# Queries and keys of the latent attention made in token rows and turned on TensorE, with the key products between the two halves of the value products

## What is computed

```python
def mla_shared_kv(h, w_kv_a, kv_a_norm, w_kv_b, k_nope_norm, k_rope_norm, cos, sin):
    ckv = h @ w_kv_a
    c_kv = rms_norm(ckv[..., :256], kv_a_norm)
    k_rope = apply_rope(rms_norm(ckv[..., 256:], k_rope_norm), cos, sin)
    kv = (c_kv @ w_kv_b).reshape(bsz, seq, 16, 64 + 64)
    k_nope, v = rms_norm(kv[..., :64], k_nope_norm), kv[..., 64:]
    k = concatenate([k_nope, broadcast_to(k_rope, (bsz, seq, 16, 32))], -1)
...
def mla_queries(h, w_q_a, q_a_norm, w_q_b, q_nope_norm, q_rope_norm, cos, sin):
    c_q = rms_norm(h @ w_q_a, q_a_norm)
    q = (c_q @ w_q_b).reshape(bsz, seq, 16, 64 + 32)
    q = concatenate([rms_norm(q[..., :64], q_nope_norm),
                     apply_rope(rms_norm(q[..., 64:], q_rope_norm), cos, sin)], -1)
...
s = q_block @ k.T / sqrt(96);  p = softmax(causal(s));  o = p @ v
```

## Time and profile before

| | us |
|---|---|
| median of three runs | 1800.92 (1800.91 to 1801.32) |
| the profiled execution's own time | 1800.97 |
| its span, first to last instruction | 1799.2 |
| first query product of the attention stage starts | 599.46 |
| first transpose of probabilities of head 0 | 629.96 |
| last score block (head 15) starts its causal term | 767.22 |

### The profile page before, as it was taken

The page is one execution under the profiler, slowest core; times in us unless marked ns, Lnnn a source line. Parts: engine busy times, 40 slices in busy tenths (PEclk is TensorE's granted clock), DMA queues, the critical chain, the costliest instruction groups (busy, mean ns, idle before and its releaser), DMA issues.

```text
span 1799.2 us, 27385 instructions
## 1 busy us (share of the span) xinstructions
PE 1755.8 (98%) x10262; PEld 1417.5 (79%) x10262; DVE 1234.6 (69%) x1863; ACT 931.8 (52%) x1668; POOL 488.0 (27%) x383
## 2 busy tenths in 40 slices
PE   9999999999999999999999999999999999999997
PEld 6778799999887656678999988778666777866675
DVE  8964488887446677758888835465676576567657
ACT  6634466654224677646566522232567633366763
POOL 0870267674000000006776600122000213200010
PEclk9999999999999999999999999999999999999999
DMA  6322322323333111122323233333111133312111
GB/s 217 91 90 82 94 95 95 118 95 118 95 97 95 40 32 29 59 82 72 117 95 118 93 117 89 96 96 97 59 59 48 48 93 100 101 47 59 49 60 56
DMA packets 58799, 152.64 MB, mean 85 GB/s; under 512 B 17024, under 2 KB 22048, under 8 KB 58672
## 3 DMA queue, kind: packets, MB, share of 16 engines
q1 hardware_dynamic: 55120, 148.24, 26.5%
q0 software_dynamic: 3552, 2.70, 0.6%
HBM read 143.76 MB, written 4.19 MB: 82 GB/s over the span
## 4 chain that ended last, share of the span: by engine, by line
PE 84%; DVE 6%; ACT 4%; POOL 3%; issue 2%; DMA 0%; SPq 0%; ACTq 0%; DVEq 0%; POOLq 0%
PE bank L2420 11%; PE bank L2421 11%; PE bank L2422 11%; PE bank L2633 8%; PE bank L2635 7%; PE bank L2634 7%; PE bank L2989 3%; PE bank L2991 3%; PE bank L2990 3%; PE bank L2942 2%; PE bank L2971 2%; PE bank L2972 2%; PE bank L2973 2%; PE bank L2713 1%; DVE wl L1532 1%
## 5 line engine op out<-in xcount | busy, mean ns | idle before, releaser
L1532 DVE TENSOR_TENSOR wl<-raw,wh 128x1024 fp32r<-128x1024 f32 (+3 forms) x199 | 234.1, 1176 | 271.3 <-ACT wh L831 266.9
L831 ACT ACTIVATE wh<-raw 128x1024 fp32r<-128x1024 f32 (+3 forms) x199 | 193.0, 970 | 354.1 <-PE bank L2422 287.6
L2420 PE MATMUL bank<-hidH,wh 128*128 128x512 f32 x352 | 137.4, 390 | 0.0
L2421 PE MATMUL bank<-hidL,wh 128*128 128x512 f32 x352 | 137.0, 389 | 0.0
L2422 PE MATMUL bank<-hidH,wl 128*128 128x512 f32 x352 | 136.9, 389 | 0.0
L2633 PE MATMUL bank<-xH,wh 128*128 128x256 f32 x480 | 135.8, 283 | 0.0
L2634 PE MATMUL bank<-xL,wh 128*128 128x256 f32 x480 | 135.8, 283 | 0.0
L2635 PE MATMUL bank<-xH,wl 128*128 128x256 f32 x480 | 135.8, 283 | 0.0
L2989 PE MATMUL bank<-xH,wh 128*128 128x512 f32 x256 | 111.3, 435 | 5.9 <-ACT qk L1395 3.1
L742 POOL TENSOR_TENSOR raw<-raw,wsum 128x512 f32<-128x512 f32 x40 | 86.6, 2164 | 110.9 <-DVE wl L1861 110.9
L2991 PE MATMUL bank<-xH,wl 128*128 128x512 f32 x256 | 100.8, 394 | 0.0
(11 more groups left out here) (522 smaller groups left out, 5210.8 us busy)
## 6 DMA issues: line engine op xcount, KB each, us to landing
raw<-w_gu_dram SPq DMA_DIRECT2D x88, 512.0 KB, 3.7
raw<-w_p_dram SPq DMA_DIRECT2D x64, 512.0 KB, 3.6
raw<-w_dn_dram SPq DMA_DIRECT2D x32, 448.0 KB, 3.4
raw<-w_glu_dram SPq DMA_DIRECT2D x16, 512.0 KB, 3.6
raw<-w_dn_dram SPq DMA_DIRECT2D x16, 512.0 KB, 3.7
raw<-w_out_dram SPq DMA_DIRECT2D x16, 512.0 KB, 3.5
raw<-w_in_dram SPq DMA_DIRECT2D x8, 512.0 KB, 7.7
raw<-w_o_dram SPq DMA_DIRECT2D x8, 512.0 KB, 3.6
```

Of the source, the lines that this page charges most:

```text
L831: nc.scalar.activation(wh[:, (st.base + u) % 2, 0:kts * P], raw[:, (st.base + u) % 4, 0:kts * P], ACT.Copy).then_inc(w_high, 1)
L1532: nc.vector.tensor_tensor(wl[:, s, 0:kts * P], raw[:, (st.base + u) % 4, 0:kts * P], wh[:, s, 0:kts * P].bitcast(F32), ALU.subtract).then_ ...
L2420: nc.tensor.matmul(bank, wh[:, s, w], hi[:, k, :], start=first and kt == 0, stop=False)
L2421: nc.tensor.matmul(bank, wh[:, s, w], lo[:, k, :], start=False, stop=False)
```

## The change

The queries and keys are made with the tokens down the partitions. `unit(n)` on TensorE makes one of 32 units in the order of `UNITS`: a part and a block `t` of 128 tokens. The parts are n0 to n3 (the plain dimensions of four heads, 256 columns), r0 and r1 (the 32 rotated dimensions of eight heads, 256 columns) and k0, k1 (the plain keys of eight heads, 512 columns). The exchanged copy of the rotated dimensions isn't computed any more: VectorE writes it out of order instead. A unit is squared by ScalarE (`unit_square`), summed over each head's dimensions along the row by VectorE (`unit_sums`), its roots of 128x4 or 128x8 words are made by ScalarE (`root_of_unit`), and VectorE multiplies them in while it copies the unit to `q_rows` or `k_rows` (`scale_unit`, one instruction for n and k, three for r). `turn_queries(h)` and `turn_keys(pair)` then turn a head's or pair's four 128x128 pieces on TensorE into bank 7, from where VectorE makes `qst` (`take_queries`, one multiply with the table) and ScalarE makes `kst` (`take_keys`, two instructions of 64 rows).

Fourteen units stand ahead of the loop: n0 and r0 before the values, k0 between `values(3)` and `values(4)`, one of n1 before the scores of head 0 and one among them. The other 18 stand in heads 0 to 9: 3, 3, 2, 2, 2, 2, 1, 1, 1, 1. The matrix constants for the two other means are gone, the blocks of the stage are ten instead of 26, the key weights are stored row by row, and the two tables `qtab` are made earlier on VectorE, between `take_latent(2)` and `take_latent(3)`.

```diff
+BLOCKS_B = [("q", 0), ("q", 1), ("v", 0), ("k", 0), ("v", 1), ("q", 2), ("q", 3), ("k", 1), ("q", 4), ("q", 5)]
+UNITS = [(part, t) for part in (("n", 0), ("r", 0), ("k", 0), ("n", 1), ("r", 1), ("k", 1), ("n", 2), ("n", 3)) for t in range(QT)]
+for _h, _n in enumerate((3, 3, 2, 2, 2, 2, 1, 1, 1, 1)):
...
+            def root_of_unit(n):
+                act.wait_ge(sem("unit_summed"), n + 1)
+                inverse_root(unit_root[:, n % 2, 0:groups], unit_sum[:, n % 2, 0:groups], ...)
...
                 for j in range(QT):
                     if j < 3:
                         copy_turned(h, j)
                     if h + 1 < NH:
                         probs(h + 1, 1 - s, j)
+                    if 1 <= j <= len(units):
+                        root_of_unit(units[j - 1])
+                        ahead_of_unit(units[j - 1])
+                    if j < len(units):
+                        unit_square(units[j])
...
+                for to, of in copies:
+                    nc.vector.tensor_tensor(to, of, root.to_broadcast(list(of.shape)), ALU.mult).then_inc(sem("unit_scaled"), 1)
...
+            def unit(n):
+                before = n - 4 if n < 3 * QT + 2 else n - 2
+                if before >= 0:
+                    pe.wait_ge(sem("unit_scaled"), SCALED[before])
+                for kt in range(kts):
+                    w = slice(kt * wide, (kt + 1) * wide)
+                    nc.tensor.matmul(o, hi[:, kt, rows], wh[:, b % 2, w], start=kt == 0, stop=False)
+                    nc.tensor.matmul(o, hi[:, kt, rows], wl[:, b % 2, w], start=False, stop=False)
+                    ins = nc.tensor.matmul(o, lo[:, kt, rows], wh[:, b % 2, w], start=False, stop=kt == kts - 1)
...
-            head_queries(0)
+            for n in range(QT):
+                unit(n)
             latent_mean(2)
+            for n in range(QT, 2 * QT):
+                unit(n)
...
             for h in range(NH):
                 if h + 2 < NH:
-                    head_queries(h + 2)
+                    turn_queries(h + 2)
...
-                    if j == 1 and h + 2 < NH:
-                        query_mean(h + 2)
+                    if j < len(units):
+                        unit(units[j])
...
+                if s and pair + 2 < NH // 2:
+                    turn_keys(pair + 2)
```

More of the change, by code:

```diff
@@ L2056, in share_first @@
                     share_probs(h, j)
[L2058 to L2060 removed]
+            unit_sums(0)
+            for n in range(1, 2 * QT):
+                unit_sums(n)
+                if n == 4:
+                    ahead(st, 0, 0, True)
+                scale_unit(n - 1)
+                if n == 5:
+                    normalise(range(5, 6))
+                    nc.vector.tensor_tensor(T[:, 3, :], latent(5), ropeT[:, :], ALU.mult).then_inc(sem("krope_part"), 1)
+            scale_unit(2 * QT - 1)
+            ahead(st, 0, 1, True)
+            dve.wait_ge(sem("krope_folded"), 1)
+            rope_rows(0)
+            take_queries(0)
+            ahead(st, 0, 2, True)
+            unit_sums(2 * QT)
+            for n in range(2 * QT + 1, 3 * QT):
+                unit_sums(n)
+                scale_unit(n - 1)
+            scale_unit(3 * QT - 1)
+            take_queries(1)
+            ahead(st, 0, 3, True)
+            unit_sums(3 * QT)
             row_least(0, 0)
+            rope_rows(1)
             row_least(0, 1)
[L2063 to L2064 removed]
+            scale_unit(3 * QT)
             row_least(0, 2)
             ahead(st, 0, 4, True)
[L2067 to L2068 removed]
+            unit_sums(3 * QT + 1)
             row_least(0, 3)
[L2070 to L2071 removed]
             def output_low(pair):
@@ L2087, in _ @@
                     row_least(h + 1, 1)
+                for n in units[0:1]:
+                    unit_sums(n)
                 take_sums(h, slice(3, 4))
@@ L2091, in _ @@
                     output_low(pair - 1)
-                if s == 0 and 1 <= pair < NH // 2 - 1:
-                    head_keys(pair + 1)
                 if h + 2 < NH:
-                    head_queries(h + 2)
-                if s and pair + 2 < NH // 2:
-                    ahead(st, 0, AT_B["k", pair + 2], True)
+                    take_queries(h + 2)
+                for n in units[1:2]:
+                    scale_unit(n - 1)
+                    ahead_of_unit(n - 1)
+                    unit_sums(n)
                 if h + 1 < NH:
@@ L2100, in _ @@
                 copy_turned(h)
+                for n in units[2:3]:
+                    scale_unit(n - 1)
+                    ahead_of_unit(n - 1)
+                    unit_sums(n)
                 if h + 1 < NH:
                     row_least(h + 1, 3)
+                for n in units[-1:]:
+                    ahead_of_unit(n)
+                to_scale = units[-1:]
             def add_to_x(name, after):
@@ L2844, in _ @@
             pe.wait_ge(evicted, tiles["b"] + 4)
+            values(0)
+            values(1)
             values(2)
+            turn_queries(0)
             values(3)
+            for n in range(2 * QT, 3 * QT):
+                unit(n)
+            turn_queries(1)
             values(4)
             values(5)
+            turn_keys(0)
+            unit(3 * QT)
+            turn_keys(1)
             scores(0, 0)
```

312 lines of the change are left out of this document (166 added, 146 removed).

## The result

The change makes the kernel slower: **1822.78 us** median (1821.19 to 1825.6) against 1800.91 (1800.52 to 1801.32) for the kernel before on the same chip, a ratio of 1.0123 with a 95% interval of 1.0106 to 1.0141. The profiled execution took 1823.03 us, with a span of 1821.2. That is 20.8 us over the forecast of 1802.2 and outside its range. Behind the attention stage the program takes as long as before.

The account below looks back on a forecast made before the run. TensorE, busy 98% of the span, was taken as the bound. Heads 6 to 13 gain 15.8 us, heads 0 to 5 lose 7, the entry 9, head 14 1: +1.2 on 1800.97, 1802.2 us, range 1796 to 1809.5.

Parts of the forecast that it names:

- the rival of the short rows: VectorE's short-row passes in the units cost 0.15 us more each, giving 1809.5 us; chance 0.2.
- The estimate of 98 ns: Spacing of 256-column query matmuls from the skill page, meaning a 2.3 us loss; the prediction set it aside for the trace's 0.12.
- first T0: First probabilities turn of head 0, forecast to start at 639.0 where it was 629.96, +9.0 us.
- heads 0 to 13, order: Head lengths counted from the engines' queues, from 12.6 us (head 1) to 5.75, sum 122.9 us.
- The gap between heads: From S3 to the next T0: 1.4 us, formerly filled by a 2.13 us product, now by a 0.44 turn, leaving 0.9.
- The clock rival: TensorE's clock falls to its lower level in one head, doubling 5 to 8 us of matmuls: 1808 us; chance 0.05.
- further waits: Rival: waits the hand count leaves out, mostly ScalarE's, at 0.3 us a head give 5 us: 1807; chance 0.1.
- Ahead of the loop: Entry before the first T0, which comes 9.0 us later: mostly work moved ahead, some 4 us new waits.
- wait at `fold`: Ahead of the loop, TensorE waits 2.1 us for the rotated part of the keys, behind five units' work on VectorE.
- Head 1: Longest head at 12.6 us, with VectorE waiting for ScalarE's `wh` before `wl`; TensorE has 7.9 us of work.
- The late pairs: Late heads at 7.5 us (even) and 5.75 (odd, VectorE-bound): 13.25 a pair against 18.76.
- The relief of 20.3 us: TensorE in the changed stage: 68.2 us of work removed, 47.9 added, the gain if TensorE stayed the bound.

Follow-up runs that it names:

- the filled run: Changed kernel plus 84 unread 512-column matmuls on TensorE ahead of the waiting query turn at heads 2, 4, 6, 8, 10 and 12; 1814.66 us.
- the turn moved: Changed kernel with TensorE's turn of a later head's query rows behind the next head's second scores instead of ahead of T0; 1816.21 us.
- the low part moved alone: Changed kernel with VectorE's low part of a weight block between the next head's first and second row extremes, not behind this head's fourth; 1823.25 us.
- both waits moved: Changed kernel with the query turn behind the second scores and VectorE's low part between the next head's row extremes; 1802.27 us, ratio 1.0006.
- Taking part of that out as well: Query turn and low part moved, plus later fold, first probabilities block ahead of fourth row extreme, key turns and ScalarE's key copy earlier; 1798.33 us, ratio 0.9985.

## Why the prediction was wrong, step by step

**The work and its prices were right, but for one.** A unit's matmuls of 256 columns stand 0.12 us apart, those of 512 columns 0.23. VectorE's and ScalarE's new forms, groups of the change's trace from 590 to 800 us:

```profile
L2093 DVE TENSOR_TENSOR q_rows<-bank,unit_root 128x256 f32<-128x256 f32 x24 | 10.0, 417 | 1.5 <-ACT unit_root L890 1.5
...
L2093 DVE TENSOR_TENSOR k_rows<-bank,unit_root 128x512 f32<-128x512 f32 x8 | 5.5, 683 | 0.0
...
L2093 DVE TENSOR_TENSOR q_rows<-bank,unit_root 128x128 f32<-128x128 f32 x16 | 3.8, 279 | 0.0
...
L2075 DVE TENSOR_REDUCE unit_sum<-unit_sq 128x4 f32<-128x256 f32 x8 | 3.3, 411 | 1.8 <-ACT unit_sq L1239 1.8
```

The forecast took 0.42, 0.69, 0.29 and 0.42 us for these four. The pair of roots takes 0.5. So the rival of the short rows is out. The one price too low is `take_keys`: 1.0 us a pair in the prediction, two copies of 0.68 us in the trace (1.38 together).

The estimate of 98 ns for 256 columns, worked out in the prediction from the figures of the Trainium skill, "TensorE: Matmul & The Clock Gate", section "Back-to-back issue gap" (256 is a third of the way from 128 to 512 columns, not half), is not borne out by the units' 0.12 us either.

**The sum of the miss.** The forecast had the last causal term's end at 768.8. It starts at 789.40 with a pitch of 0.46, so it ends at 789.86, 21.1 later:

| step | forecast | measured | miss | shown by |
|---|---|---|---|---|
| first T0 | 639.0 | 641.50 | 2.5 | 1.5 of it clock |
| heads 0 to 13, clock | 0 | 8.8 | 8.8 | the filled run, 133.33 against 142.09 |
| heads 0 to 13, order | 122.9 | 133.3 | 10.4 | the turn moved |
| the rest, to head 14's last causal term | 6.9 | 6.3 | -0.6 | |

**"The gap between heads" is the step that failed.** It let "one turn of 0.44" fill 1.4 us before T0 and left 0.9. At the even-to-odd gaps that is right (0.75 of idle time). At the odd-to-even ones the filler itself waited 3.0 to 4.45 us. Moving it behind S1 gives heads 3, 5, 7, 9 and 11 of 10.59, 9.95, 7.16, 8.28 and 5.73 us, where the forecast had 10.65, 10.05, 7.2, 8.35 and 5.75. In the filled run, where the turn stays, they take 11.69, 11.38, 9.39, 9.71 and 7.97. So **8.1 of the 10.4 us of order are this one wait** (50.1 against the forecast's 42.0), and everything else in those heads had been counted well. The other 2.3 are small: head 13 takes 6.69 us in the filled run against 5.75, head 1 13.23 against 12.6, and the seven even heads together 63.3 against 62.5. The prediction saw half of it: it named `take_keys` "before the first copies of the next head", and so asked what it would delay on ScalarE's queue, not what it ends. It took the wait of `turn_queries` on `kv_used` into account nowhere, nor that `unit_scaled` there means, at heads 6 and 10, a unit made in the head just before.

**The clock rival was sized at one head and given a chance of 0.05.** It decided 8.8 us in the heads and 1.5 ahead of them, half of the miss. The forecast's own path had it at nothing. In the heads it came behind the waits of 3 to 4.5 us, and not as 5 to 8 us in one head but as 1.3 to 2.0 us in each of five. The argument against it, 15.70 of 19 us busy at 1.00, is about a stretch in which idle time is spread out, and head 1, at 8.24 of 13.26 busy, kept its clock too. What fell was the clock of the head after. A busy share averaged over a head did not tell it; the length of a single idle stretch told more, though not surely, as the last section shows. The two rivals were also not independent: further waits bring the clock with them, and their 5 and 6 us should have stood in one case.

**Ahead of the loop.** The wait at `fold` was forecast at 2.1 us and is 1.73. In this execution the granted clock from 612 to 618 is 0.72. The run with the low part moved alone has the same instructions there at 1.00, and its T0 starts at 639.95. So 1.5 of the 2.5 us are the clock, and the count by hand was 1.0 short. The other runs agree: T0 starts at 641.3 to 641.8 in the five with 0.72 there and the same work up to T0, and at 639.96 in the one other with 1.00.

**Head 1** took 13.26 us against 12.6, with VectorE waiting 2.0 us for `wh`, as said. On its own that wait did not hold TensorE, however: taking it away alone changed nothing, since the query turn waited as long. The late pairs, forecast at 13.3, took 17.3 and 15.6 (heads 10 and 11, 12 and 13), and heads 0 to 5 took over 9.5 each, as the forecast wanted.

**What stands behind it all.** The relief of 20.3 us of TensorE work could not be had while chains of two other engines end at the start of a head. With both waits moved, the kernel is level with the one before, not below it: 1.0 to 1.5 us of idle time remain ahead of nearly every T0, where a product of 2.13 us had covered the row extreme, the exponentials and the scaling. Taking part of that out as well gave 1798.33. Even there the entry stays dear: T0 of head 0 starts at 638.62, 8.7 us later than before, and from it to the last causal term the heads take 126.0 us in place of 137.3, so that only 2.6 us are left.

## What to carry to other kernels

An instruction that is to fill a gap must be looked up for its own waits first. In an in-order queue a filler with a late input can be worse than the gap, as all behind it waits along: here waits of 3.0 to 4.45 us stand where the forecast had 0.9. Where two waits of like length end at the same point, each tried alone shows little (6.6 and 0 us here) and both together show all (20.5), so a null result for one edit does not clear its cause. A change that empties the busiest engine in pieces should carry the clock in the forecast wherever one wait grows to some us: filling such waits with useless matmuls gave 8.1 us back and is a quick way to weigh it.

## What the runs showed of the hardware

The granted clock drops to the lower of its two levels (1.2 GHz against 2.4) behind five of the six idle times of 3.0 to 4.45 us, and the trace shows it after the wait, in the work that follows: matmuls of 512 columns stand 0.43 us apart (0.23 otherwise). The stretches of the change around the wait ahead of head 2:

```profile
661.00:664.00 3.00, 0.00 (x0) 0.00 (x0) 0.99 (x2) 2.75 (x7) 0.00 (x0) 1.00 0.00 0
664.00:667.00 3.00, 2.44 (x11) 2.28 (x12) 2.11 (x9) 1.16 (x4) 0.00 (x0) 0.67 0.55 175
667.00:670.00 3.00, 3.00 (x13) 2.35 (x13) 0.64 (x2) 1.05 (x3) 0.00 (x0) 0.77 0.00 0
670.00:673.00 3.00, 3.00 (x16) 1.34 (x15) 2.72 (x6) 1.45 (x6) 0.00 (x0) 1.00 0.00 0
```

It is not certain at a given length. Behind 3.02 us ahead of head 8 it stayed at 1.00, behind 3.02 ahead of head 12 it fell. The same idle time of 2.73 us ahead of head 1, with the same instructions on both sides, was followed by 0.50 in one kernel (the turn moved) and by 1.00 in another (turn and low part moved):

```profile
651.60:655.00 3.40, 3.07 (x15) 3.07 (x16) 1.88 (x7) 1.71 (x7) 0.00 (x0) 0.50 0.42 151
```

```profile
651.60:655.00 3.40, 3.39 (x28) 3.34 (x29) 2.43 (x10) 2.37 (x11) 0.00 (x0) 1.00 0.35 131
```

Shorter waits were not safe either. Behind 2.26 us ahead of head 1 the change's trace stays at 1.00, and behind 2.25 us in the run with the low part moved alone the same matmuls run at 0.50 for the next 3.3 us. The wait of 1.73 us at the fold was followed, from 612 to 618, by 0.72 in the change's trace and five others, by 0.64 in one and by 1.00 in three. The four runs of the change spread over 4.4 us, the four of the kernel before over 0.8. What tips it from one execution to the next was not settled, and that this causes the spread is argued, not shown.
